# Copying the gate rows of two token groups out of two neighbouring PSUM banks with one ScalarE instruction

## The chip, the cores and the metric

The kernel runs on one core of one Trainium2 chip. The metric is the device time of one execution in microseconds; the kernel before took 1968.15 us, the median of 3 runs (1967.19 to 1974.01). The engines are named as in the profile: PE (TensorE, matrix products), ACT (ScalarE), DVE (VectorE), POOL (GpSimd) and SP (the engine that issues most DMAs).

## The reference, cut to what matters

The kernel is one step of one layer of a decoder: a gated delta net and a pooling branch, and then a mixture of 16,384 small experts called PEER. It has 512 prompt tokens and 32 sample tokens. The change lies in PEER alone:

```
scores = einsum('thpd,hpnd->thpn', q, sub_keys)       # 8 heads, 2 halves, 128 keys each
s_top, i_top = top_k(scores, 16)                       # per half
best, sel = top_k(all 256 sums of a pair of halves, 16)
idx   = i_top[half 0] * 128 + i_top[half 1]            # 8 * 16 = 128 experts a token
gates = softmax(best)
act   = gelu(einsum('td,tkd->tk', x, expert_u[idx]))
out   = einsum('tk,tkd->td', gates * act, expert_v[idx])
```

For the first 384 prompt tokens the kernel doesn't gather the chosen experts. It computes all 128 x 128 of them for every token, and multiplies by a gate matrix that is zero where an expert wasn't chosen. For one token that matrix is (128 x 128): entry (i, j) is the sum, over the token's 128 choices, of gate times [first half's key is i] times [second half's key is j].

## The kernel before, in words

The gate matrices are made in three rounds (`u` = 0, 1, 2) of 128 tokens each. A round is 32 *quads* of four tokens. This text numbers the quads of all rounds from 0 to 95, so round 1 begins at quad 32 and round 2 at quad 64. For one quad:

- DVE writes `hot_b` (choices x keys, a 1 where the second key matches, four tokens in one instruction, L2833).
- `hot_a` (gate where the first key matches) is written token by token by three engines. In an even quad POOL does two tokens, DVE one and ACT one; in an odd quad POOL does one, DVE one and ACT two (`shares`, L2312).
- ACT needs two instructions for a token: `away` = |iota - key| (L2708), then `hot_a` = relu(gate - large * away) (L2717). Before the second it waits until the first has finished (L2715).
- PE multiplies the two for each of the four tokens into bank `q % 4` of the PSUM tensor `dd` (L2559; each profile row of a quad counts 8 matmuls). It waits for the three writers, and (L2556) until the quad four before has been read out of its bank.
- ACT copies the bank, 128 x 512 numbers, into `gstage`, a buffer in SBUF for eight quads (L2731). SP then stores it to DRAM.

Between two quads PE works on something else, its *pieces*: parts of the product of the tokens with `expert_u` (L2228), about two pieces (6 matmuls) after each quad. Eight pieces make a chunk, and 24 chunks are computed in this stage. When a chunk is done, ACT does `early_gelu`: it waits for the chunk (`done`), rounds the weights of the chunk after the next (`w_hi`, L437, 128 x 1024), and takes the gelu (L2241, 128 x 384).

The order on each engine is the order of the code; nothing is scheduled. ACT runs through steps q = 0 to 33 of a round (`beside_choice`, L2701): first the `away` of quad q, then the copy of quad q - 2 (`store_row`), then `early_gelu` if quad q - 2 is one of those after which a chunk is complete (`E_AT`), then `hot_a` of quad q. Chunks complete after quads 3, 7, 11, ..., 43 (so that the gelu falls in an odd step) and then after 46, 50, 54, ..., 90 (in an even step) and 93. In step 17 of each round ACT also takes the exponentials of the next choice (L2664), which loads another table; the next gelu loads the old one again.

All this has to be over before PE's later stage of dense products can use `dd` (L2621). That stage goes to the end of the kernel.

Of the kernel before, what the change touches and what calls it, by code (L numbers as in the profile page):

```python
# [11 lines left out]
ACT = mybir.ActivationFunctionType  # L12
# [59 lines left out]
HOTS = 4  # L72
# [92 lines left out]
def build(nc, x_in, c_in, vec_in, cst_in, wba_in, ada_in, stream_in, v_in, urow_in, conv_in, pool_in, delta_in,  # L165
          wpool_in, keys_in, wout_in, y_out, conv_out, delta_p_out, delta_s_out, pool_out):
    with ExitStack() as ctx:
# [5 lines left out]
        def sem(name):  # L173
            assert name not in names
            names.add(name)
            lasting = name in LASTING
            s = nc.alloc_semaphore(name)
            if not lasting:
                phase_sems.append(s)
            return s  # L180
# [102 lines left out]
        def at(name, offset, shape, dt=F32):  # L283

            return nc.alloc_sbuf_tensor_at(name, shape, dt, offset=base + offset)
# [75 lines left out]
        gstage = [at(f"gstage{s}", (72 + 16 * s) * K, [P, P, TB]) for s in range(2)]  # L361
# [29 lines left out]
        dd = ctx.enter_context(nc.psum_tensor("dd", [P, 4, 512], F32))  # L391
# [1815 lines left out]
        TQ = P // 4  # L2207
# [6 lines left out]
        for i in range(E_HEAD, NE):  # L2214
            q = next(q for q in range(n_quads) if e_upto[q] >= (i - E_HEAD + 1) * KC)
# [19 lines left out]
        def early_gelu(act, i):  # L2235
            k = Chunk(C_EARLY + i)
            done(act, k)
            split_hi(act, k + 2)
            if i >= 2:
                act.wait_ge(e_stored[i % 2], 16 * (i // 2))  # L2240
            nc.scalar.activation(ge_st[i % 2][:], pp[k.slot][:, 0, 0:TD], ACT.Gelu).then_inc(pp_read[k.slot], 1)  # L2241
# [10 lines left out]
        def top16(dve, st, src, spare, values, index, n, beside=lambda: None):  # L2252
# [25 lines left out]
        gcols_ready, hots_vector, hots_pool, hots_scalar, away_done, quad_done, quad_read = (  # L2278
            sem("gcols_ready"), sem("hots_vector"), sem("hots_pool"), sem("hots_scalar"), sem("away_done"),
            sem("quad_done"), sem("quad_read"))  # L2280
# [4 lines left out]
        NQ = TB // 4  # L2285
# [26 lines left out]
        def shares(q):  # L2312
            return ((2, 1, 1), (1, 1, 2))[q % 2]
# [30 lines left out]
        with nc.Block() as block:  # L2344
# [287 lines left out]
            def _(act):  # L2632
# [28 lines left out]
                def exponents(p):  # L2661
                    act.wait_ge(ex_in, p + 1)
                    of = best[:, 0:SG if ORDER[p] == SPARSE_S else H]
                    nc.scalar.activation(of, of, ACT.Exp).then_inc(ex_out, 1)  # L2664
# [36 lines left out]
                def beside_choice(u):  # L2701
                    for q in range(TQ + 2):
                        if q < TQ:
                            own = range(4 * q + 4 - shares(q)[2], 4 * q + 4)
                            act.wait_ge(gcols_ready, u + 1)
                            act.wait_ge(quad_done, u * TQ + (q + 1))
                            for n, c in enumerate(own):
                                nc.scalar.activation(away[:, (aways[0] + n) % 4, :], iota, ACT.Abs,  # L2708
                                                     bias=gcols[u % 2][:, 0, c:c + 1], scale=-1.0).then_inc(away_done, 1)
                        if q >= 2:  # L2710
                            store_row(u, q - 2)
                            for i in E_AT.get(u * TQ + (q - 2), ()):
                                early_gelu(act, i)
                        if q < TQ:
                            act.wait_ge(away_done, aways[0] + len(own))  # L2715
                            for n, c in enumerate(own):
                                last = nc.scalar.activation(hot_a[:, (q % HOTS) * 4 + c % 4, :],  # L2717
                                                            away[:, (aways[0] + n) % 4, :], ACT.Relu,
                                                            bias=gcols[u % 2][:, 2, c:c + 1],
                                                            scale=gcols[u % 2][:, 3, c:c + 1])  # L2720
                            last.then_inc(hots_scalar, 1)
                            aways[0] += len(own)
                        if q == EXP:
                            exponents(u + 2)

                def store_row(u, q):
                    s, b = (q // NQ) % 2, q // NQ
                    if q % NQ == 0:
                        act.wait_ge(gates_st[s], u * 32 + (16 * (b // 2) + 16))
                    act.wait_ge(quad_done, u * TQ + (q + HOTS + 1))  # L2730
                    nc.scalar.activation(gstage[s][:, :, 4 * (q % NQ):4 * (q % NQ) + 4],  # L2731
                                         dd[:, q % 4, :].rearrange("p (j t) -> p j t", t=4),
                                         ACT.Copy).then_inc(quad_read, 1)

                for s in range(4):
                    act.wait_ge(turn_st[s], 16 * 2)
                for u in range(ND):
                    beside_choice(u)
# [425 lines left out]
```

## Time and profile before

| | |
|---|---|
| median of 3 runs | 1968.15 us |
| profiled execution, its own time | 1972.14 us |
| its span (first to last instruction) | 1970.2 us |
| busy PE, DVE, ACT, POOL | 1891.4, 1560.5, 857.0, 758.3 us |
| quad stage | about 829 to 1047 us |
| copies L2731 | 96, of which the median takes 584 ns |

Busy time is the time in which an engine executes; several instructions of one engine can overlap at their ends, so that the sum of their durations is more than their busy time. In a row of the timeline the two numbers at the start are the start and the duration in us of a run of equal instructions; what stands in brackets is how long the engine stood idle before it, and the instruction that seems to have released it.

### The profile page before, as it was taken

The page shows a single profiled execution, that of the slowest core. Times are in us where ns is not written, and L with a number is a line of the kernel's source. Part 1 is how long each engine was busy: PE and PEld are TensorE (multiplying, and loading weights), DVE is VectorE, ACT ScalarE, POOL GpSimd, SP SyncE. Part 2 cuts the span into 40 slices and gives each one's busy share as a digit, 9 for nine tenths or more (in the row PEclk, how much of TensorE's full clock was granted, in tenths as well). Part 3 has the DMA queues.
Part 4 walks back from the last instruction along what each step waited for, and adds up shares of the span by engine and source line. Part 5 has one row for each costly group of instructions (what it writes and reads, how often), then busy time and mean ns, then how long its engine had stood idle before and what let it go on. Part 6 is the DMA issues. An engine that isn't in the chain of part 4 may idle for free.

```text
span 1970.2 us, 33663 instructions
## 1 busy us (share of the span) xinstructions
PE 1891.4 (96%) x12681; PEld 1709.6 (87%) x12681; DVE 1560.5 (79%) x3013; ACT 857.0 (43%) x1473; POOL 758.3 (38%) x579
## 2 busy tenths in 40 slices
PE   5989999999999999889999999999999999999997
PEld 3679999999977899889898888888888888888886
DVE  4466777777766788998895888888888898888887
ACT  3334444444434235488995333333333333333333
POOL 0010000000024433787891444445444555555570
PEclk8989999999999999999999999999999999999999
DMA  8822222222272324755778999999999999999983
GB/s 361 327 60 72 79 71 71 72 70 65 81 280 74 141 65 152 242 159 163 213 207 301 343 354 374 367 360 372 367 374 353 366 363 362 349 356 374 343 302 137
DMA packets 176129, 470.00 MB, mean 239 GB/s; under 512 B 16353, under 2 KB 75585, under 8 KB 172641
## 3 DMA queue, kind: packets, MB, share of 16 engines
q1 hardware_dynamic: 129888, 300.06, 43.4%
q0 software_dynamic: 46080, 167.79, 22.8%
q8 instruction: 102, 1.67, 0.3%
q14 instruction: 59, 0.48, 0.1%
HBM read 424.21 MB, written 43.58 MB: 237 GB/s over the span
## 4 chain that ended last, share of the span: by engine, by line
PE 52%; DVE 11%; POOL 1%; issue 1%; ACT 1%; DVEq 0%; ACTq 0%
PE pp L2590 19%; PE dd L2603 18%; PE pp L2603 9%; PE pp L2228 3%; PE dd L2559 3%; POOL hot_a L2373 1%; DVE top_i L2271 1%; DVE top_i L2260 1%; DVE less L2261 1%; DVE top L2811 1%; DVE top_v L2255 1%; DVE top_v L2266 1%; DVE cand L2921 1%; PE pp L453 1%; DVE hot_b L2833 1%
## 5 line engine op out<-in xcount | busy, mean ns | idle before, releaser
L437 ACT ACTIVATE w_hi<-w_raw 128x1024 fp32r<-128x1024 f32 x202 | 212.6, 1052 | 142.1 <-PE pp L453 100.2
L453 PE MATMUL pp<-act_hi,w_hi 128*128 128x272 f32 x1056 | 240.6, 310 | 9.0 <-DVE act_lo L758 4.4
L2590 PE MATMUL pp<-act_hi,w_hi 128*128 128x384 f32 x712 | 241.5, 339 | 1.7 <-DVE acc L3068 1.7
L2590 PE MATMUL pp<-act_lo,w_hi 128*128 128x384 f32 x712 | 239.9, 337 | 0.0
L2590 PE MATMUL pp<-act_hi,w_lo 128*128 128x384 f32 x712 | 239.3, 336 | 0.0
L441 DVE TENSOR_TENSOR w_lo<-w_raw,w_hi 128x1024 fp32r<-128x1024 f32 x173 | 211.5, 1223 | 25.1 <-ACT w_hi L437 25.1
L453 PE MATMUL pp<-act_lo,w_hi 128*128 128x272 f32 x1056 | 220.2, 290 | 0.0
L453 PE MATMUL pp<-act_hi,w_lo 128*128 128x272 f32 x1056 | 220.1, 290 | 0.0
L2767 ACT ACTIVATE co_hi<-cf 128x384 fp32r<-128x384 f32 x128 | 67.4, 526 | 350.1 <-PE pp L2603 295.3
L2373 POOL TENSOR_SCALAR hot_a<-cst,gcols 128x128 f32<-128x128 f32 x144 | 180.9, 1266 | 27.3 <-PE dd L2559 25.7
L453 PEld LDWEIGHTS pp<-act_hi,w_hi 128*128 128x128 f32 x1056 | 165.8, 191 | 25.3 <-issue 17.8
L3060 DVE TENSOR_TENSOR v_lo<-v_raw,v_hi 128x1024 fp32r<-128x1024 f32 x128 | 156.4, 1222 | 31.0 <-ACT v_hi L2769 31.0
L2300 POOL DMA_INDIRECT x<-in_v,idx x80 | 130.9, 1637 | 98.4 <-DVE acc L2993 90.8
L453 PEld LDWEIGHTS pp<-act_lo,w_hi 128*128 128x128 f32 x1056 | 168.3, 191 | 0.0
L453 PEld LDWEIGHTS pp<-act_hi,w_lo 128*128 128x128 f32 x1056 | 167.4, 191 | 0.0
L2603 PE MATMUL dd<-v_hi,co_hi 128*128 128x512 f32 x512 | 159.7, 393 | 1.5 <-DVE v_lo L3060 1.5
L2300 POOL DMA_INDIRECT x<-in_urow,idx x80 | 101.9, 1273 | 150.4 <-DVE junk L2985 144.2
L2603 PE MATMUL dd<-v_lo,co_hi 128*128 128x512 f32 x512 | 158.7, 391 | 0.0
L2603 PE MATMUL dd<-v_hi,co_lo 128*128 128x512 f32 x512 | 158.7, 391 | 0.0
L1001 POOL COPY conv_new<-cbuf 128x3 f32<-128x3 f32 x24 | 8.1, 337 | 386.8 <-ACT cbuf L1200 386.8
L2300 POOL DMA_INDIRECT ring<-in_v,idx x80 | 114.3, 1429 | 91.9 <-DVE acc L2993 80.1
L2300 POOL DMA_INDIRECT ring<-in_urow,idx x80 | 102.8, 1285 | 105.7 <-DVE junk L2985 102.6
(437 smaller groups left out, 4563.7 us busy)
## 6 DMA issues: line engine op xcount, KB each, us to landing
w_raw<-in_stream SPq DMA_DIRECT2D x206, 512.0 KB, 5.0
v_raw<-in_v SPq DMA_DIRECT2D x128, 512.0 KB, 6.4
ada_w<-in_ada SPq DMA_DIRECT2D x24, 1024.0 KB, 12.0
gt<-gate_matrix SPq DMA_DIRECT2D x31, 768.0 KB, 8.3
gate_matrix<-gstage SPq DMA_DIRECT2D x11, 2048.0 KB, 9.9
early<-cst SPq DMA_DIRECT2D x38, 192.0 KB, 4.2
cst<-early SPq DMA_DIRECT2D x38, 192.0 KB, 10.3
wrow<-in_wout SPq DMA_DIRECT2D x8, 512.0 KB, 8.1
```

The source lines that it names most:

```text
L437: nc.scalar.activation(w_hi[k.slot][:], w_raw[k.slot][:], ACT.Copy).then_inc(w_hi_done, 1)
L441: nc.vector.tensor_tensor(w_lo[k.slot][:], w_raw[k.slot][:], w_hi[k.slot][:].bitcast(F32), ALU.subtract).then_inc(w_lo_done, 1)
L453: last = nc.tensor.matmul(pp[s][:, b, 0:HN], w[:, c * P:(c + 1) * P], a[:, c, b * HN:(b + 1) * HN], start=(c == 0 and w is w_hi[s] and a i ...
L2228: last = nc.tensor.matmul(pp[s][:, 0, 0:TD], w[:, c * P:(c + 1) * P], a[:, c, 0:TD], start=(c == 0 and w is w_hi[s] and a is act_hi), stop ...
L2255: st(nc.vector.max(values(j)[:, 0:8], src(j)))
L2300: nc.gpsimd.indirect_dma_start(out=ring[n % RING][:], out_offset=None, in_=tables[kind], in_offset=bass.IndirectOffsetOnAxis(ap=idx_of[whi ...
L2373: last = nc.gpsimd.tensor_scalar(hot_a[:, (q % HOTS) * 4 + o, :], iota, gcols[u % 2][:, 0, c:c + 1], gcols[u % 2][:, 2, c:c + 1], ALU.is_e ...
L2559: last = nc.tensor.matmul(dd[:, q % 4, o::4], hot_a[:, v, :], hot_b[:, v, :], start=True, stop=True)
L2590: last = nc.tensor.matmul(pp[s][:, 0, 0:TD], w[:, c * P:(c + 1) * P], a[:, c, 0:TD], start=(c == 0 and w is w_hi[s] and a is act_hi), stop ...
L2603: last = nc.tensor.matmul(accs[t][half], co[:, cols], v[:, half * 512:(half + 1) * 512], start=(b == 0 and co is co_hi[0] and v is v_hi[0] ...
L2767: nc.scalar.activation(co_hi[e % 2][:], cf[e % 2][:], ACT.Copy).then_inc(c_hi_done, 1)
L3060: nc.vector.tensor_tensor(v_lo[e % 2][:], v_raw[e % 2][:], v_hi[e % 2][:].bitcast(F32), ALU.subtract).then_inc(v_lo_done, 1)
```

## The change

`store_row` becomes `store_rows`. It is called in odd steps only, and copies quads q - 3 and q - 2 of that step at once: 128 x 1024 numbers from two neighbouring banks. It waits for the later of the two quads, and its semaphore counts two. In even steps nothing is copied. The 96 copies of 512 become 48 of 1024. Since a line is inserted, L2717 is L2718 in the changed kernel, and the copy, L2731, is L2733.

```diff
                         if q >= 2:
-                            store_row(u, q - 2)
+                            if q % 2:
+                                store_rows(u, q - 3)
                             for i in E_AT.get(u * TQ + (q - 2), ()):
                                 early_gelu(act, i)
...
-                def store_row(u, q):
+                def store_rows(u, q):
                     s, b = (q // NQ) % 2, q // NQ
                     if q % NQ == 0:
                         act.wait_ge(gates_st[s], u * 32 + (16 * (b // 2) + 16))
-                    act.wait_ge(quad_done, u * TQ + (q + HOTS + 1))
-                    nc.scalar.activation(gstage[s][:, :, 4 * (q % NQ):4 * (q % NQ) + 4],
-                                         dd[:, q % 4, :].rearrange("p (j t) -> p j t", t=4),
-                                         ACT.Copy).then_inc(quad_read, 1)
+                    act.wait_ge(quad_done, u * TQ + (q + 1 + HOTS + 1))
+                    at = slice(4 * (q % NQ), 4 * (q % NQ) + 8)
+                    nc.scalar.activation(gstage[s][:, :, at].rearrange("p j (two t) -> p two j t", two=2),
+                                         dd[:, q % 4:q % 4 + 2, :].rearrange("p two (j t) -> p two j t", t=4),
+                                         ACT.Copy).then_inc(quad_read, 2)
```

How ACT's order changes in an even step and the odd step behind it, where a gelu falls in the odd one (quads 40 and 41). `away` and `hot_a` are the two instructions of a token, `gstage<-dd` is the copy, `w_hi` and `cst<-pp` belong to `early_gelu`. Before:

```order
L2708 ACTIVATE away<-cst,gcols_159 128x128
L2731 ACTIVATE gstage_164<-dd 128x128x4
L2717 ACTIVATE hot_a<-away,gcols_159 128x128
L2708 ACTIVATE away<-cst,gcols_159 128x128 x2
L2731 ACTIVATE gstage_164<-dd 128x128x4
L437 ACTIVATE w_hi<-w_raw 128x1024
L2241 ACTIVATE cst<-pp 128x384
L2717 ACTIVATE hot_a<-away,gcols_159 128x128 x2
```

The same two steps on ACT after the change:

```order
L2708 ACTIVATE away<-cst,gcols_159 128x128
L2718 ACTIVATE hot_a<-away,gcols_159 128x128
L2708 ACTIVATE away<-cst,gcols_159 128x128 x2
L2733 ACTIVATE gstage_164<-dd 128x2x128x4
L437 ACTIVATE w_hi<-w_raw 128x1024
L2241 ACTIVATE cst<-pp 128x384
L2718 ACTIVATE hot_a<-away,gcols_159 128x128 x2
```

The copy between `away` and `hot_a` of the even step is gone; the copy ahead of `w_hi` and `hot_a` of the odd step is twice as large.

Where the gelu falls in the even step (quads 56 and 57), before, on ACT:

```order
L2708 ACTIVATE away<-cst,gcols_159 128x128
L2731 ACTIVATE gstage_164<-dd 128x128x4
L437 ACTIVATE w_hi<-w_raw 128x1024
L2241 ACTIVATE cst<-pp 128x384
L2717 ACTIVATE hot_a<-away,gcols_159 128x128
L2708 ACTIVATE away<-cst,gcols_159 128x128 x2
L2731 ACTIVATE gstage_164<-dd 128x128x4
L2717 ACTIVATE hot_a<-away,gcols_159 128x128 x2
```

And after:

```order
L2708 ACTIVATE away<-cst,gcols_159 128x128
L437 ACTIVATE w_hi<-w_raw 128x1024
L2241 ACTIVATE cst<-pp 128x384
L2718 ACTIVATE hot_a<-away,gcols_159 128x128
L2708 ACTIVATE away<-cst,gcols_159 128x128 x2
L2733 ACTIVATE gstage_164<-dd 128x2x128x4
L2718 ACTIVATE hot_a<-away,gcols_159 128x128 x2
```

Here the copy in front of `w_hi` is gone, and the odd step behind it has the large one in front of its two `hot_a`. On the other engines the order of instructions is the same as before.

## Rows read from the trace of the kernel before

**Rows 1.** Windows: busy us (x instructions) of each engine, PEclk, DMA share, GB/s.
```profile
core 0: us, PE busy (x) PEld busy (x) DVE busy (x) ACT busy (x) POOL busy (x), PEclk, DMA share, GB/s
829.00:1047.00 218.00, 198.15 (x1353) 192.39 (x1354) 188.14 (x516) 190.89 (x439) 182.97 (x146) 0.97 0.67 195
1047.00:1900.00 853.00, 851.27 (x4187) 760.46 (x4186) 726.29 (x916) 301.09 (x414) 419.94 (x304) 1.00 0.96 358
```

**Rows 2.** Waits in the quad stage, 829 to 1047: total us, times, longest.
```profile
ACT gstage L2731 <- PE dd L2559: 17.4, 28, 3.8
PE dd L2559 <- ACT hot_a L2717: 10.6, 12, 2.1
PEld dd L2559 <- DVE hot_a L2837: 9.6, 10, 2.4
PE dd L2559 <- POOL hot_a L2373: 7.5, 2, 5.3
```

**Rows 3.** ACT's groups: busy us, mean ns, then idle before (page and window).
```profile
L2767 ACT ACTIVATE co_hi<-cf 128x384 fp32r<-128x384 f32 x128 | 67.4, 526 | 350.1 <-PE pp L2603 295.3
...
L2731 ACT ACTIVATE gstage<-dd 128x512 f32<-128x512 f32 x95 | 55.8, 587 | 18.0 <-PE dd L2559 17.4
L437 ACT ACTIVATE w_hi<-w_raw 128x1024 fp32r<-128x1024 f32 x24 | 25.4, 1059 | 7.9 <-PE pp L2228 7.8
```

**Rows 4.** The copy L2649 out of two banks, min/median/max ns.
```profile
L2649 ACT ACTIVATE qt<-pp x16: 606/608/633, 636.5 to 750.3; 128x544 f32<-128x544 f32 x16
```

**Rows 5.** Timeline, ACT's step for quad 13, and PE's quad 13.
```profile
859.87 0.60 ACT L2731 ACTIVATE gstage<-dd 128x512 f32<-128x512 f32 x1 [0.39 <-PE dd L2559]
861.00 1.06 ACT L437 ACTIVATE w_hi<-w_raw 128x1024 fp32r<-128x1024 f32 x1 [0.54 <-PE pp L2228]
...
862.34 0.86 ACT L2717 ACTIVATE hot_a<-away,gcols 128x128 f32<-128x128 f32 x2
...
863.46 1.13 PE L2559 MATMUL dd<-hot_b,hot_a 128*128 128x128 f32 x8 [0.63 <-ACT hot_a L2717]
```

**Rows 6.** Timeline, ACT's step for quad 41.
```profile
926.39 0.60 ACT L2731 ACTIVATE gstage<-dd 128x512 f32<-128x512 f32 x1 [0.39 <-PE dd L2559]
927.00 1.06 ACT L437 ACTIVATE w_hi<-w_raw 128x1024 fp32r<-128x1024 f32 x1
...
928.34 0.87 ACT L2717 ACTIVATE hot_a<-away,gcols 128x128 f32<-128x128 f32 x2
```

**Rows 7.** Timeline, ACT's step for quad 57, and PE's quad 57.
```profile
963.49 0.58 ACT L2731 ACTIVATE gstage<-dd 128x512 f32<-128x512 f32 x1
963.96 0.87 ACT L2717 ACTIVATE hot_a<-away,gcols 128x128 f32<-128x128 f32 x2
...
965.28 1.05 PE L2559 MATMUL dd<-hot_b,hot_a 128*128 128x128 f32 x8
```

**Rows 8.** Timeline, ACT's step for quad 32 (no copy in it).
```profile
908.52 0.39 ACT L2708 ACTIVATE away<-cst,gcols 128x128 f32<-128x128 f32 x1
908.94 0.49 ACT L2717 ACTIVATE hot_a<-away,gcols 128x128 f32<-128x128 f32 x1
```

**Rows 9.** Timeline around the start of round 2: ACT, and PE's quad 64.
```profile
978.99 0.59 ACT L2731 ACTIVATE gstage<-dd 128x512 f32<-128x512 f32 x1
979.47 0.40 ACT L2708 ACTIVATE away<-cst,gcols 128x128 f32<-128x128 f32 x1
...
980.72 1.13 PE L2559 MATMUL dd<-hot_b,hot_a 128*128 128x128 f32 x8 [1.25 <-ACT hot_a L2717]
```

**Rows 10.** Timeline, ACT's step for quad 85 and PE's quad 85.
```profile
1023.85 0.88 ACT L2717 ACTIVATE hot_a<-away,gcols 128x128 f32<-128x128 f32 x2
...
1025.17 1.05 PE L2559 MATMUL dd<-hot_b,hot_a 128*128 128x128 f32 x8
```

**Rows 11.** Windows after two long waits of PE (columns as in rows 1).
```profile
911.00:913.00 2.00, 2.00 (x8) 2.00 (x8) 1.78 (x3) 1.78 (x5) 1.72 (x2) 0.50 0.00 0
955.00:957.00 2.00, 1.99 (x14) 2.00 (x15) 1.95 (x3) 2.00 (x6) 1.15 (x2) 1.00 1.08 313
```

## The prediction

> **What bounds the kernel now.** I first read a table of windows [rows 1]. From 1047 us to 1900 PE is busy 851.27 of 853 us, so whatever the quad stage loses or gains arrives at the end of the kernel unchanged. In the quad stage, 829 to 1047, PE is busy 198.15 of 218 us. The 19.9 us in which it stands still are all that a change of ACT's work can win there, apart from the clock. ACT is busy 190.89 of these 218 us, as much as any engine, so it looks as if ACT's copies were worth cutting.
>
> Then the waits [rows 2]. PE waits for ACT's `hot_a` 12 times, 10.6 us; 9.6 us stand against DVE's `hot_a` and 7.5 against POOL's. Comparing the ends of the three writers of a quad with the start of its matmuls, the DVE entries are those of the weight load of the same quads, for which the matmul row names ACT, and DVE was done 4 to 6 us before; of POOL's, 5.3 us are the first quad, and the other is ACT's too. So apart from the start of the stage it is always ACT's `hot_a` that ends PE's wait. ACT in turn waits 17.4 us for PE before its copies [rows 2] and 7.9 us for PE's pieces before `w_hi` [rows 3]. This isn't a full engine: it is a loop between PE and ACT, and what counts is the path from a quad's end to the `hot_a` two quads later, not ACT's sum.
>
> Last the timeline of one such loop [rows 5]. The copy of quad 11 starts at 859.87. `w_hi` starts at 861.00, not behind the copy but when PE's pieces are done: ACT stood idle 0.54 us. Gelu and two `hot_a` follow, these end at 863.20, and PE starts 0.26 us later, having waited 0.63 us. Without a gelu the step is shorter and PE doesn't wait. 0.25 us from the end of `hot_a` to PE is the least that occurs; whatever a quad has beyond it I call its slack.
>
> **The new instruction's price.** A copy of 512 numbers takes 587 ns [rows 3]. The trace has no copy of 1024 out of PSUM. The nearest is one of 544 out of two banks, 608 ns [rows 4], so two banks in one instruction cost nothing extra. From 384 to 1024 numbers ACT goes from 526 to 1059 ns, 0.83 ns a number [rows 3]; 512 more are 0.43 us, and the pair takes 1.01 us. Bounds: 0.98 us by the 0.75 ns between 512 and 544 numbers, and 1.17 us, two single copies, if nothing is saved. I take 1.01, since both slopes are near it.
>
> In duration 48 x (2 x 0.587 - 1.01) = 7.9 us go. But ACT starts its next instruction before the last has ended: from copy to `hot_a` it is 963.96 - 963.49 = 0.47 us [rows 7]. In ACT's row of work a single copy weighs 0.47 and a pair 0.47 + 0.43 = 0.90. A pair saves 0.04 us by itself. And the single copy stood between `away` and the `hot_a` that needs it. Where nothing stands there, `hot_a` comes 908.94 - 908.52 = 0.42 us behind `away` [rows 8], against 0.29 from one to the next otherwise (the copy of rows 7 follows the second `away` so). So the even step without gelu gets 0.29 + 0.47 - 0.42 = 0.34 us shorter, the odd step 0.43 longer: per pair 0.09 us more. In ACT's own row of work nothing is won.
>
> The Trainium skill, page "ScalarE: Activation LUTs", section "What ACT_TABLE_LOAD costs", has an ACTIVATE with immediate scale and bias at 186 ns + 0.833 ns a number, and 93 ns of it overlapping with the neighbour. By that each pair saves 93 ns, 48 of them 4.5 us, where ACT's work is the bound. The trace agrees on the slope and is below it for 512 numbers (587 against 612 ns); the start it leaves over is 0.04 us, not 0.09.
>
> **What it costs, place by place.** In an even step no wait for quad q - 2 is left unless a gelu stands there, so that `hot_a` is early; PE doesn't need it earlier, since it waited in such quads only behind a gelu. In an odd step `hot_a` is 0.43 us later. Hidden or not, by kind:
>
> 1. Gelu in the odd step, chunk done with the last piece (quads 5, 9, 13, 17, 21, 25 and 95). The 0.54 us in which ACT stands idle before `w_hi` [rows 5] cover the 0.43. Cost 0.
> 2. Gelu in the odd step, chunk done one piece earlier (quads 29, 37, 41, 45, and the start of round 1, quad 32). `w_hi` now starts 0.61 us behind the copy's start, without idle time [rows 6]; with the pair it's 0.90 to 0.91. So 0.30 us at each. 29 has 0.18 us of slack and pays 0.12. Sum 4 x 0.30 + 0.12 = 1.3 us.
> 3. Gelu in the even step: `w_hi` waits for the pieces anyway, so this `hot_a` stays. The odd step behind it is late by the earlier gelu: `hot_a` ends at 964.83, PE starts at 965.28 [rows 7], so the slack is 0.45 - 0.25 = 0.20. It pays 0.43 - 0.20 = 0.23. Quads 57, 61, 69 do so; 73, 77, 89, 93 have 0.03 more slack. Sum 3 x 0.23 + 4 x 0.20 = 1.5 us.
> 4. Start of round 2, quad 64. The copy of quad 63 stands between the gelu and the round's first `away`, 0.48 us [rows 9]. Now the pair stands there: 0.43 us, all of it, as PE waits 1.25 us for that `hot_a`.
> 5. The three stretches with table loads (quads 17 to 21, 49 to 53, 81 to 85). ACT runs without a pause, and by the 0.34 and 0.43 above I follow each `hot_a`: -0.1 us in the first, 0.1 in the second, where slack takes most, and in the third 0.15 us at quad 84 and 0.43 - 0.19 more at quad 85, whose slack is 1025.17 - 1024.73 - 0.25 [rows 10]: 0.4. Sum 0.4 us. With no slack at all it would be 1.3.
>
> Everywhere else the odd step has over 0.43 us of slack. PE's wait for `quad_read` moves by a step at most, and always lies before a `hot_a` for which PE waits anyhow. The last pair of the stage ends 0.4 us later; PE has about 8 us of products in front of its first write to `dd`. SP's store of eight quads leaves 0.4 us later, and its buffer is wanted a group of quads later. DVE and POOL wait for PE and have 1.5 us or more in nearly all quads.
>
> Sum: 1.3 + 1.5 + 0.4 + 0.4 = 3.6 us, with 1.17 for the pair 16 places more by up to 0.16, some 6.2; with all of it hidden, 0. The profiled execution would go from 1972.1 to 1975.8 us. The median of the runs is 4.0 us below its own profiled execution; the same sum on it gives 1971.8 us.
>
> **Rivals.**
>
> - *All hidden*: the slack is larger than I read it, for instance since ACT's wait for the earlier quad of a pair costs something that now goes. Then 1968.2 us. For it: 17.4 us of ACT idle time before the copies [rows 2]. Against: none of it is behind a gelu, where PE waits.
> - *ACT's work is the bound*: each copy that goes is worth its share, 0.04 to 0.16 us times 48, at most 7.9 us; 1960.3 to 1966. For it 190.89 us busy of 218 [rows 1]. Against: the idle times of ACT in the same loop. The skill's 4.5 us lie here, at 1963.7.
> - *PE passes ahead, and the clock stays up*: the early even `hot_a` shorten the long waits. After 2.14 and 2.11 us of idle PE (quads 21, 32) the granted clock was 0.50, the lower level of 1.2 GHz (the window at 911 in [rows 11]), at some 1.6 us each; half of PE's 19.9 us and both of these would be 13 us, 1955. Against: these two waits end behind a gelu in an odd step and don't get shorter.
> - *Slower, by the clock*: after the waits of 1.83, 1.62 and 1.25 us at quads 52, 84 and 64 the clock stayed 1.00 (the window at 955 in [rows 11]). If the pair takes clearly over 1.17 us, so that these waits come near 2.1 us, three more falls cost 4.8 us, and 16 places at 0.2 or more another 3.2 beside my 3.6: 1980 us. It decides from about 1.3 us for the pair on. Against: rows 4.
>
> The forecast has 0.55, all hidden 0.15, ACT the bound 0.16, the clock kept up 0.05, slower by the clock 0.09. Only differences over 0.5%, 9.8 us, can be told from no change here. Faster by that: 0.05; slower: 0.09; within: 0.86. The range takes in hidden and most of ACT as the bound below, and the pair at 1.17 us with some spread of the measurement above: 1962 to 1977 us.
>
> **What would show it.** The copies should be 48 at 0.98 to 1.05 us; over 1.2 the last rival is right. Between `away` and `hot_a` of an even step 0.42 us. In the windows the quad stage should be 3 to 5 us longer than 218, and the stage after it the same. PE's wait at quad 13 stays 0.63 us, at quad 41 it grows by 0.3, at quad 64 to about 1.7; quad 57 starts 2.25 us after quad 56 instead of 2.03. If ACT's wait times before copies vanish and the stage is shorter, ACT was the bound. I am wrong altogether if the time leaves 1958 to 1978 us, or if PE's waits are ended by DVE or POOL.

## The result, and the profile after

The changed kernel takes 1975.29 us, the median of 15 runs (1973.8 to 1980.58), against 1969.01 us of the kernel before, also 15 runs (1967.19 to 1974.01). The ratio is 1.0029, 95% interval 1.0021 to 1.0037: 5.7 us slower. Timed a second time, beside the experiments below (e3_after_again), it was 1.0024 (1.0012 to 1.0035). That is inside the 0.5% called no change, and it is slower all the same: the interval doesn't reach 1. The profiled execution took 1975.85 us with a span of 1974.0.

The windows of the changed kernel, to be read against [rows 1]; the columns are the same:

```profile
829.00:1047.00 218.00, 197.89 (x1337) 187.93 (x1338) 187.08 (x514) 188.45 (x388) 185.69 (x146) 0.98 0.65 191
1051.00:1900.00 849.00, 848.14 (x4175) 758.62 (x4175) 723.74 (x914) 301.89 (x414) 418.77 (x303) 1.00 0.95 357
```

The stage of dense products is as full as before, and starts 4 us later. ACT has fewer instructions in the quad stage and is busy 188.45 us in place of 190.89; PE has done 16 matmuls fewer by 1047 us. The waits of the changed kernel in the quad stage, taken up to 1051 us since the stage now ends later, where before there were [rows 2], and its copy, where before there was L2731 in [rows 3]:

```profile
PEld dd L2559 <- issue: 27.8, 28, 6.0
ACT gstage L2733 <- PE dd L2559: 19.7, 16, 6.7
PE dd L2559 <- ACT hot_a L2718: 11.2, 14, 2.5
PE dd L2559 <- POOL hot_a L2373: 9.3, 5, 5.8
...
L2733 ACT ACTIVATE gstage<-dd 128x1024 f32<-128x1024 f32 x48 | 48.9, 1019 | 21.2 <-PE dd L2559 19.7
```

The pair takes 1019 ns where 1.01 us was forecast. ACT's waits before its copies are fewer (16 for 28) but in sum longer, and PE's waits for ACT are more (14 for 12). The row "issue" of PE's weight load (PEld, the load that has to be done before a quad's matmuls) has grown; before it was:

```profile
PEld dd L2559 <- issue: 17.4, 11, 5.5
```

So with 28 entries for 11 the weight load comes a little late in many more quads. The profile finds no releaser for that; the timeline does. Quad 41 of the changed kernel, ACT's step and then PE, against [rows 6]:

```profile
926.26 1.02 ACT L2733 ACTIVATE gstage<-dd 128x1024 f32<-128x1024 f32 x1 [0.70 <-PE dd L2559]
927.18 1.05 ACT L437 ACTIVATE w_hi<-w_raw 128x1024 fp32r<-128x1024 f32 x1
...
928.50 0.88 ACT L2718 ACTIVATE hot_a<-away,gcols 128x128 f32<-128x128 f32 x2
...
929.63 1.13 PE L2559 MATMUL dd<-hot_b,hot_a 128*128 128x128 f32 x8 [0.47 <-ACT hot_a L2718]
```

`w_hi` starts 0.92 us behind the copy's start; it was 0.61. The copy itself also starts a little later behind the quad that it waits for, quad 39. PE's rows of that quad, before and after:

```profile
925.30 1.05 PE L2559 MATMUL dd<-hot_b,hot_a 128*128 128x128 f32 x8
...
925.11 1.05 PE L2559 MATMUL dd<-hot_b,hot_a 128*128 128x128 f32 x8
```

The single copy started 926.39 - 925.30 = 1.09 us behind that [rows 6], the pair starts 1.15 us behind it. Together that makes `w_hi` 0.36 to 0.37 us later. Quad 57, against [rows 7] (quads 56, 57 and 58 of PE are the last three rows):

```profile
964.26 1.01 ACT L2733 ACTIVATE gstage<-dd 128x1024 f32<-128x1024 f32 x1
965.16 0.88 ACT L2718 ACTIVATE hot_a<-away,gcols 128x128 f32<-128x128 f32 x2
...
964.02 1.13 PE L2559 MATMUL dd<-hot_b,hot_a 128*128 128x128 f32 x8 [0.25 <-ACT hot_a L2718]
966.30 1.13 PE L2559 MATMUL dd<-hot_b,hot_a 128*128 128x128 f32 x8
968.32 1.05 PE L2559 MATMUL dd<-hot_b,hot_a 128*128 128x128 f32 x8
```

From copy to `hot_a` it is 0.90 us, as forecast, and quad 57 starts 2.28 us behind quad 56 where it was 2.03. PE can start only 0.26 us after `hot_a` has ended at 966.04. The row of quad 57 shows no wait, since the matmul follows its late weight load; only the interval gives it away. And quad 58 comes 2.02 us behind 57 where it was 1.94. The start of round 2, against [rows 9]:

```profile
980.48 1.02 ACT L2733 ACTIVATE gstage<-dd 128x1024 f32<-128x1024 f32 x1
981.38 0.40 ACT L2708 ACTIVATE away<-cst,gcols 128x128 f32<-128x128 f32 x1
...
982.64 1.13 PE L2559 MATMUL dd<-hot_b,hot_a 128*128 128x128 f32 x8 [1.68 <-ACT hot_a L2718]
```

PE's wait grew from 1.25 to 1.68 us, the 0.43 forecast.

**The part that the order decides.** To compare kernels closer than whole executions allow, I took the start of each quad's first matmul (L2559, 8 matmuls a quad) and compared the 95 intervals with those of a second profile of the kernel before (e4_before_again). The intervals up to quads 1 to 3 are left out, and those up to the two quads behind each wait of over 1.9 us in that kernel's own profile, since the clock may be low there. (Single intervals are compared below by the quad at their end.) In the two profiles of before this sum agrees within 0.01 us, in the two of the changed kernel it is 4.89 and 4.85 us more. I call it the order part. So it leaves out what a kernel's long waits cost through the clock. From quad 95 to the end the profiles here agree within 0.15 us (924.22 to 924.37), but for e9 with 924.92.

### The profile page after: what moved, and what is told of

It reads as the page before. It is cut to its first block, busy times and chain, and to the rows that moved or that the text cites. A ratio compares the mean times of both kernels' runs of the same rounds, so it can differ in the third digit from the quotient of the medians.

```text
span 1974.0 us, 33651 instructions
## 1 busy us (share of the span) xinstructions
PE 1894.8 (96%) x12681; PEld 1708.0 (87%) x12681; DVE 1561.0 (79%) x3013; ACT 857.3 (43%) x1425; POOL 760.2 (39%) x579
## 4 chain that ended last, share of the span: by engine, by line
PE 60%; POOL 2%; DVE 2%; ACT 2%; issue 1%; DVEq 0%; ACTq 0%; POOLq 0%
PE pp L2590 19%; PE dd L2603 18%; PE pp L2603 9%; PE pp L2228 5%; PE pp L453 4%; PE dd L2559 3%; POOL hot_a L2373 2%; PE dd L2489 1%; POOL w_lo L2245 1%; ACT w_hi L437 0%; ACT hot_a L2718 0%; DVE hot_b L2835 0%; DVE fin_x L3021 0%; PE dd L1720 0%; PE dd L2533 0%
```

## The experiments

Each was timed against the kernel before on the same chip. e4_before_again is a single run, there for its profile, to which the others are compared. The order part is from one profile of each.

| kernel | ratio to before, 95% | order part, us |
|---|---|---|
| before, its first profile | - | +0.01 |
| e4_before_again | 1966.01 us, one run | 0 |
| the change | 1.0029 (1.0021 to 1.0037) | +4.89 |
| e3_after_again | 1.0024 (1.0012 to 1.0035) | +4.85 |
| e1_two_singles | 1.0017 (1.0007 to 1.0027) | +4.56 |
| e2_pair_even | 1.0011 (1.0003 to 1.0020) | +2.16 |
| e5_pair_last | 1.0013 (1.0004 to 1.0021) | +1.94 |
| e6_dose_odd | 1.0063 (1.0050 to 1.0076) | +11.82 |
| e10_dose_even | 1.0050 (1.0036 to 1.0064) | +7.90 |
| e7_gelu_last | 0.9920 (0.9907 to 0.9933) | -13.43 |
| e11_gelu_last_again | 0.9915 (0.9902 to 0.9929) | -13.52 |
| e8_gelu_last_pair | 0.9932 (0.9919 to 0.9945) | -10.32 |
| e9_both_last | 0.9923 (0.9910 to 0.9937) | -13.52 |

**Two single copies in the changed order.** Against the changed kernel, with `store_row` again as it was before:

```diff
                             if q % 2:
-                                store_rows(u, q - 3)
+                                store_row(u, q - 3)
+                                store_row(u, q - 2)
```

> The order of the changed kernel (copies in odd steps alone, two quads at a time), but with two copies of 512 numbers, one behind the other, in place of one of 1024. Theory of the place (what costs is that the copying of both quads stands ahead of the two hot_a of an odd step): the two copies weigh 0.94 us there, the pair about 0.91, so the stage is about 0.5 us longer than with the pair, 4 to 6 us longer than before; ratio to before 1.002 to 1.004. Theory of the instruction (two banks and a four-dimensional pattern in one instruction cost something of their own): back to within 1 us of before, ratio 1.000.

Measured: slower than before as the theory of the place says, if a little under its range, so an order without any pair costs the same kind of time. But it isn't slower than the pair, it is 0.3 us faster in the order part. ACT's step for quad 45 in e1 shows why:

```profile
930.05 0.57 ACT L2733 ACTIVATE gstage<-dd 128x512 f32<-128x512 f32 x1
930.92 0.60 ACT L2733 ACTIVATE gstage<-dd 128x512 f32<-128x512 f32 x1 [0.30 <-PE dd L2559]
931.53 1.06 ACT L437 ACTIVATE w_hi<-w_raw 128x1024 fp32r<-128x1024 f32 x1
```

The first copy doesn't wait for the later quad; it is over when that quad is done, and `w_hi` is 0.61 us behind the second, as before the change. The five places of kind 2 cost nothing in e1 and 1.7 us in the change. In the odd steps of kind 3 e1 pays 0.29 and 0.25 us where the change pays 0.24 and 0.20: there the pair is really 0.05 us cheaper, which is all that its missing start is worth. Between quads 49 and 54 e1 is 0.8 us behind the change, 0.6 of it at quad 50, which wasn't traced further.

**The pair in the even steps.** Against the changed kernel:

```diff
+                        if q % 2 == 0 and u * TQ + q >= 4 and q < TQ:
+                            store_rows((u * TQ + q - 4) // TQ, (q - 4) % TQ)
+                        if u == ND - 1 and q >= TQ:
+                            store_rows(u, TQ - 4 + 2 * (q - TQ))
                         if q >= 2:
-                            if q % 2:
-                                store_rows(u, q - 3)
```

> The pair in one instruction as in the changed kernel, but moved to the even steps: in an even step quads q-4 and q-3 are copied, across the ends of rounds too, and nothing in odd steps. Theory of the place: an even step has one away and one hot_a of ACT in place of two, and no wait for quad q-2 is left, so PE finds hot_a in time in quads 57, 61, 69, 73, ... and w_hi is ready by PE's pieces in quads 29 to 45; also nothing is copied on the path into quad 64. The stage gets 4.5 to 6 us shorter than with the change and 0 to 1 us shorter than before; ratio to before 0.9990 to 1.0000. Theory of the instruction: still 3 to 6 us slower than before.

The sites named are gone: quads 29, 37, 41, 45, 57, 61, 69, 73, 77, 89 and 93 are within 0.05 us of before. So the instruction isn't what costs there. But the sum of +2.16 us misses my 0 to -1, and the ratio, 1.0011, lies above the 0.9990 to 1.0000 expected. ACT's step for quad 32 in e2, against [rows 8]:

```profile
906.97 0.39 ACT L2708 ACTIVATE away<-cst,gcols 128x128 f32<-128x128 f32 x1
907.26 1.01 ACT L2735 ACTIVATE gstage<-dd 128x1024 f32<-128x1024 f32 x1
908.16 0.49 ACT L2720 ACTIVATE hot_a<-away,gcols 128x128 f32<-128x128 f32 x1
```

I had carried a pair over the end of the round, into the one step that had held no copy, and that is on the path: 0.76 us at quad 32 and 0.28 at quad 64. Nearly all of the other 1.1 us is at quads 18, 50, 52, 82 and 84, in the stretches with table loads, where ACT is behind.

**The same two kernels again.**

> The changed kernel once more, on the same chip and with the same runs of before as the others. Both theories: 3.5 to 7 us slower than before, ratio 1.002 to 1.0035. The theory that part of the difference is only when the clock falls: another profile shows quads 21 to 22 at 3.58 us again, and the stage 1.6 us longer than in the first profile.

> The kernel before once more, for a second profile of it. If the falls of the clock behind quads 21 and 32 belong to the order of work, both are there again and the stage lasts 213.0 us from quad 0 to quad 95 within 0.3; if they come by chance, one or the other is missing and the stage is 1.6 us shorter for each.

The order part came back to 0.04 us and 0.01 us. The falls of the clock didn't: behind quad 21 the first profile of before has one, and none of the other three has; behind quad 32 the first profile of before and both of the change have one, and before_again has none, with the same 2.11 us of wait as the first. The second profile of the change had none behind quad 21 either, where the expectation had one. Windows of 2 us behind these waits, in the change (quads 21 and 32) and in before_again (quad 32):

```profile
884.00:886.00 2.00, 2.00 (x17) 2.00 (x16) 0.95 (x2) 1.93 (x5) 1.29 (x1) 1.00 0.99 241
912.00:914.00 2.00, 2.00 (x11) 2.00 (x11) 1.63 (x10) 0.30 (x1) 1.45 (x2) 0.52 0.32 57
```
```profile
908.00:910.00 2.00, 2.00 (x17) 2.00 (x17) 2.00 (x11) 1.87 (x6) 2.00 (x2) 1.00 0.16 33
```

**The pair behind `hot_a`.** Against the changed kernel:

```diff
+                        if q >= TQ and q % 2:
+                            store_rows(u, q - 3)
                         if q >= 2:
-                            if q % 2:
-                                store_rows(u, q - 3)
...
                             last.then_inc(hots_scalar, 1)
                             aways[0] += len(own)
+                        if 2 <= q < TQ and q % 2:
+                            store_rows(u, q - 3)
```

> The pair in one instruction, in the odd steps, but behind the two hot_a of the step in place of ahead of them (in the two steps that end a round, where there is no hot_a, it stays ahead of the gelu). Theory of the place: the 0.2 us at quads 57, 61, 69, 73, ... and the 0.35 at 37, 41, 45 go, since these hot_a stand behind no copy; 0.36 at quad 32 and 0.43 at 64 stay, and the stretches with table loads cost up to 1 us, since there ACT's work is the bound whatever its order. The part of the stage that the order decides is 1 to 2 us longer than before (4.9 with the change); ratio to before 1.0003 to 1.0012. Theory of the instruction: it stays at 4 to 6 us, as the same 48 instructions run.

As expected: +1.94 us, of them 0.36 at quad 32, 0.43 at 64 and 0.41 each at 18 and 50; all of kind 3 and the quads 29, 37, 41, 45 are back at before. The same 48 instructions, 2.9 us less in the order part. The ratio, 1.0013, lies just above the range given.

**A double dose in odd and in even steps.** In the kernel before, one copy in two is made twice (the even dose has `q % 2 == 0`):

```diff
                     act.wait_ge(quad_done, u * TQ + (q + HOTS + 1))
+                    if q % 2 == 1:
+                        nc.scalar.activation(gstage[s][:, :, 4 * (q % NQ):4 * (q % NQ) + 4],
+                                             dd[:, q % 4, :].rearrange("p (j t) -> p j t", t=4),
+                                             ACT.Copy).then_inc(dose, 1)
+                        act.wait_ge(dose, u * TQ // 2 + q // 2 + 1)
```

> The kernel before, but in odd steps the copy is made twice (the second waits for the first, to the same place), so about 0.6 us more ahead of the hot_a of every odd step, with no pair anywhere. Theory of the place: quads 57, 61, 69, 73, 77, ... pay 0.62 less their slack of 0.2, 37, 41, 45 about 0.5, 32 and 64 0.5 to 0.6, and the stretches with table loads some 3.5 us: 9 to 12 us in all, ratio 1.004 to 1.006. Quads 5, 9, 13, 17 nearly nothing. The theory that ACT's idle time covers work wherever it stands: under 3 us.

> The kernel before, with the copy made twice in the even steps in place of the odd ones (e6_dose_odd: 11.8 us in the part that the order decides). Theory of the place: behind the gelu of an even step that PE's last piece releases nothing is paid (56, 60, 68); 76, 80, 84, 88 and 92, whose chunk is done a piece earlier, pay 0.3 to 0.4 each, and the stretches with table loads 3 to 4 us: 4.5 to 6.5 us in all, half of the odd dose. If ACT's sum of work counts and not its place, both doses cost the same, 11 to 12 us.

The odd dose pays 0.43 at 57, 61 and 69, 0.50 at 37, 41, 45 and 32, 0.63 at 64, and nothing at 5, 9, 13, 17: as worked out, 11.82 us. The even dose costs 7.90, less but above my range. Of that, 1.2 us stand at quads 29, 41 and 45, where I expected nothing, and quads 76, 80 and 92 pay 0.70 each in place of 0.3 to 0.4. What I missed is a sum: with 0.6 us more in each even step ACT no longer catches up between two gelus. At quad 41 of e10 PE waits 0.55 us where it waited 0.11, since ACT gets to `w_hi` late and without a pause:

```profile
925.47 0.60 ACT L2737 ACTIVATE gstage<-dd 128x512 f32<-128x512 f32 x1
925.97 0.49 ACT L2718 ACTIVATE hot_a<-away,gcols 128x128 f32<-128x128 f32 x1
926.35 0.69 ACT L2709 ACTIVATE away<-cst,gcols 128x128 f32<-128x128 f32 x2
926.94 0.58 ACT L2737 ACTIVATE gstage<-dd 128x512 f32<-128x512 f32 x1
927.42 1.05 ACT L437 ACTIVATE w_hi<-w_raw 128x1024 fp32r<-128x1024 f32 x1
```

The two order parts don't leave out the same intervals, though. In e10 the waits at quads 52 and 84 have grown to 2.41 and 2.24 us, and the clock fell behind both:

```profile
959.00:961.00 2.00, 2.00 (x10) 2.00 (x9) 0.17 (x1) 1.82 (x5) 1.45 (x2) 0.50 0.51 189
...
1031.00:1033.00 2.00, 2.00 (x10) 2.00 (x9) 0.66 (x2) 1.75 (x6) 0.59 (x1) 0.50 0.79 269
```

With those four intervals left out of both kernels, the odd dose costs 10.78 us and the even one 7.90. With them in both it is 11.82 and 11.06, nearly the "both the same" of the rival. In whole executions it is 12.4 and 9.9 us, and the two 95% intervals overlap. So the place matters, by some 2.9 us of 10.8 at an even clock, but by much less than I had worked out. The dose isn't what shows that the place decides; e2, e5 and e7 are.

**The gelu behind `hot_a`.** If the loop over `w_hi` and the gelu is what PE waits for, it can be taken off the path:

```diff
-                    for q in range(TQ + 2):
+                    for q in range(TQ + (2 if u == ND - 1 else 0)):
...
-                        if q >= 2:
-                            store_row(u, q - 2)
-                            for i in E_AT.get(u * TQ + (q - 2), ()):
-                                early_gelu(act, i)
+                        if u * TQ + q >= 2:
+                            store_row((u * TQ + q - 2) // TQ, (q - 2) % TQ)
...
                             last.then_inc(hots_scalar, 1)
                             aways[0] += len(own)
+                        for i in E_AT.get(u * TQ + q - 2, ()):
+                            early_gelu(act, i)
```

> The kernel before with its single copies, but in each step the gelu (w_hi and gelu) comes behind hot_a in place of ahead of it, and the copies and gelus of a round's last quads are carried into the next round's first steps. Theory of the loop (PE's waits come from the path PE's pieces, w_hi, gelu, hot_a, PE): the waits at quads 5, 9, 13, 25, 37, 41, 45, 56, 60, 68, 32, 64 and 95 all go, 10 to 14 us, ratio 0.993 to 0.995, and the falls of the clock behind quad 32 with them; waits remain only in the stretches with table loads. The theory that ACT is full in this stage: 0 to 3 us.

> e7_gelu_last once more, on the same chip as e9_both_last: ratio to before 0.991 to 0.993, and the order part of the stage within 0.3 us of 13.4 below before.

Measured: 1954.08 us against 1969.68 of before, ratio 0.9920, and 0.9915 the second time. The order part lies in the 10 to 14 us expected, the ratio a little below the range of 0.993 to 0.995. With e9 it is the fastest kernel of this study. ACT's step for quad 13 in e7, against [rows 5], and PE's quads 13, 14 and 15, which now follow each other at 1.93 us:

```profile
855.72 0.60 ACT L2731 ACTIVATE gstage<-dd 128x512 f32<-128x512 f32 x1 [0.31 <-PE dd L2559]
856.22 0.87 ACT L2715 ACTIVATE hot_a<-away,gcols 128x128 f32<-128x128 f32 x2
856.99 1.04 ACT L437 ACTIVATE w_hi<-w_raw 128x1024 fp32r<-128x1024 f32 x1
857.94 0.47 ACT L2241 ACTIVATE cst<-pp 128x384 f32<-128x384 f32 x1
...
858.50 1.05 PE L2559 MATMUL dd<-hot_b,hot_a 128*128 128x128 f32 x8
860.43 1.05 PE L2559 MATMUL dd<-hot_b,hot_a 128*128 128x128 f32 x8
862.37 1.05 PE L2559 MATMUL dd<-hot_b,hot_a 128*128 128x128 f32 x8
```

The two `hot_a` end at 857.09, 1.4 us before PE takes them, and `w_hi` and the gelu come behind. All the waits named are gone; what is left of PE's waits between two quads is 4.5 us for 15.9 in before, at quads 18, 20, 22, 53, 82 and 85, all in the stretches with table loads or just behind them. Since behind the stage's first quad no wait over 1.9 us is left, the clock stays up too (1.00 from 840 to 1027 us), and the time falls by a little more than the order part. This edit makes two moves at once: the gelu goes behind `hot_a`, and the copies and gelus of a round's last quads go into the next round's first steps. The starts of the rounds, quads 32 and 64, where the second move takes part, account for 3.7 us of the order part; the two weren't measured apart.

**The change in that order.** e8 is e7 with `store_rows` in the odd steps ahead of `hot_a`; e9 puts it behind.

> The same order as e7_gelu_last, with the pair copied by one instruction in the odd steps, ahead of hot_a, as in the change. Theory of the place: behind a gelu in an even step hot_a of the odd step has only about 0.06 us of slack left by my working from the rows, so 0.2 us at quads 57, 61, 65, 69 and at most that later, and some 0.3 in the stretches with table loads: 1 to 2.5 us slower than e7_gelu_last. If instead ACT's row of work is the bound once the loop is gone, and a pair saves its start, it is 2 to 4 us faster than e7_gelu_last.

> The order of e8_gelu_last_pair, but the pair too behind the hot_a of its odd step (ahead of the gelu where one falls there). Theory of the place: no hot_a of an odd step stands behind a copy, so the 0.2 to 0.4 us at quads 57, 65, 69 and the like of e8_gelu_last_pair are gone; the stretches with table loads stay within 1 us of e7_gelu_last. The order part of the stage is 12.5 to 14 us below before, as in e7_gelu_last (13.4): the same time as it, ratio to before 0.991 to 0.993. The theory that the instruction for two banks costs time of its own: 1 us or more above e7_gelu_last.

e8's order part is 3.1 us above e7's, somewhat over the range; 57, 65 and 69 cost 0.35 to 0.45 us each, the rest is in the stretches with table loads. The step for quad 57, behind a gelu:

```profile
953.88 0.47 ACT L2241 ACTIVATE cst<-pp 128x384 f32<-128x384 f32 x1
954.25 0.68 ACT L2708 ACTIVATE away<-cst,gcols 128x128 f32<-128x128 f32 x2
954.83 1.01 ACT L2732 ACTIVATE gstage<-dd 128x1024 f32<-128x1024 f32 x1
955.74 0.87 ACT L2715 ACTIVATE hot_a<-away,gcols 128x128 f32<-128x128 f32 x2
...
956.86 1.13 PE L2559 MATMUL dd<-hot_b,hot_a 128*128 128x128 f32 x8 [0.18 <-DVE hot_a L2838]
```

From the end of the gelu ACT works without a pause up to the `hot_a` that ends at 956.61, 0.25 us before PE; the profile names DVE for the wait, which had written its part for quad 57 by 952.40, 4.5 us before.

e9 has -13.52 us, e7 twice -13.43 and -13.52. With the pair off the path, one instruction for two banks is worth as much as two instructions. (The order part of these leaves out only the first three intervals. Leaving out those behind quads 21 and 32 too, as for the change, gives -14.29 for e9, -13.80 and -14.22 for e7, and -11.39 for e8: the same picture.)

## Why the prediction was right, and what it sized too small

The forecast was 1971.8 us, 3.6 us more than before, within 0.5%. The direction, the path and nearly each place hold; the sum measured is 4.9 us in the order part and 5.7 (4.1 to 7.3) in the ratio, so 3.6 lies just below that interval. What was off is the size of two terms, kinds 2 and 3, and no wait or path.

- *The price of the pair*: 1.01 us forecast, 1019 ns measured; 0.90 us to `hot_a` forecast and measured. That ACT wins next to nothing in its own row of work is borne out by the 0.05 us between e1 and the change in the odd steps; e9 beside e7 agrees, but there most copies are off PE's path and a saving would hardly show. The 4.5 us that the prediction took from the Trainium skill, page "ScalarE: Activation LUTs", section "What ACT_TABLE_LOAD costs", with 93 ns a start, didn't appear: of a start no more than 0.05 us was seen. (The lower bound of 0.98 us for the pair is a slip. 0.75 ns a number gives 0.97; nothing rests on it.)
- *Kind 1*, 0 forecast: 0.10 us at quad 13 in one profile, nothing in the other.
- *Kind 2*, 1.3 us: measured 0.26 at quad 29, 0.36 at 32, and 0.35, 0.35 and 0.36 at 37, 41 and 45: 1.7. The right mechanism, 0.30 us a place forecast and 0.35 measured. The prediction took it that the pair starts when the single copy would. It starts 1.15 us behind the first matmul of the quad it waits for and not 1.09, in both profiles of the change and at all seven quads read (11, 15, 23, 27, 35, 39, 43); e1's second copies start at 1.09. Why is open. The other 0.01 to 0.02 is that `w_hi` follows the pair's start at 0.92, not 0.90, and at quad 29 there is also the 0.08 below. e1 adds what the prediction didn't name: this term isn't due to the deferred copy but to the one wait for both quads.
- *Kind 3*, 1.5 us: measured 0.32 or 0.33 at each of 57, 61 and 69, and 0.28 or 0.29 at 73, 77, 89 and 93: 2.1. The odd quad pays 0.24 and 0.20 as forecast. The term mis-sized is what follows: behind a late weight load the next quad takes 2.02 us and not 1.94. That was to be read in the intervals behind PE's waits already before the change, and I left it out: seven times 0.08 are the 0.6 us between 1.5 and 2.1. e7 shows the same from the other side. Where its order takes PE's wait away, at quads 5, 9, 13, 25, 37, 41, 45, 56, 64 and 68, the interval behind becomes 0.08 to 0.10 us shorter too.
- *Start of round 2*: 0.43 forecast and measured.
- *The stretches with table loads*, 0.4 us forecast as -0.1, 0.1 and 0.4: measured -0.2, 0.4 and 0.35, together 0.6.
- *Rivals.* All hidden: no, 4.9 us show. ACT the bound: no; the same work in another order moves the order part by 2.9 us (from e5 to the change) and by 13.4 (e7). The clock kept up: the fall behind quad 21 was missing in the change, but in before_again too, so that it wasn't the change's doing. Slower by the clock: the waits at quads 52 and 84 became shorter (1.20 and 1.24 us for 1.83 and 1.62), only that at 64 grew, to 1.68, and no fall followed.
- *What neither forecast nor rivals had*: the change also makes the wait at quad 32 longer, 2.47 us for 2.11. Behind that wait the clock fell in all five profiles in which it was 2.46 us or more (both of the change, e2, e5, e6), and in two of the four in which it was 2.11 (it fell in before and e10, and not in before_again and e1). So the change may make this fall of some 1.6 us more frequent. That would fit the 5.7 us in the ratio beside the 4.9 of the order part, but with so few profiles, and a difference inside the interval, it isn't shown.

The profiled executions alone differ by 3.7 us, which fits my sum only by chance: 4.9 of the order, 0.7 of a later start of the stage (833.6 for 832.9 us), and 1.8 less in the intervals left out, of which 1.6 is the fall of the clock behind quad 21 that only the profile of before has.

## What to carry to other kernels

- An engine that is busy nearly all of a stage isn't therefore what the stage waits for, and cutting its instructions need not help. Look first for pauses in its row: here it stood still before `w_hi`, so what counted was mostly what stands between the event it waits for and the result that others wait for. Its sum of work comes in where the pauses are used up (e10).
- One instruction for two pieces takes the later one's wait for both. If the pieces come at different times, the first would have been free (1.7 us at five places here).
- Where a queue is in order, move the work that nobody waits for soon behind the result that is waited for. That, with the last quads' work carried into the next round, was worth 15.6 us here (ratio 0.9920). No saving from fewer starts was seen beyond 0.05 us each.

## What the runs showed of the hardware beyond that

- An ACTIVATE copy out of two PSUM banks at once, 128 x 1024 with runs of four numbers, took 998 to 1027 ns in 48 cases. That is what 587 ns for 512 numbers and 0.83 ns for each further one give (1.01 us), so nothing extra shows for the second bank. But where it had waited for PE it started 0.06 us later than a single copy does.
- Where TensorE's weight load for a quad came late, by 0.04 us (quad 73) or by 0.6 (quad 13), the next quad's first matmul came 0.08 to 0.10 us late as well, 2.02 for 1.94 us a quad.
- The granted clock after the same wait of PE isn't the same in each execution. After 2.11 us at quad 32 it was 0.50 in one profile of the kernel before [rows 11] and 1.00 in another; such a fall costs about 1.6 us, a third of the effect studied here. Intervals between fixed events, away from those places, agreed within 0.05 us between two executions of a kernel, but for 0.09 to 0.16 at quads 18, 19, 21 and 52 and 0.10 at quad 13.
